# Two transformer blocks on one core: the weight halves and two token buffers placed at other addresses in SBUF

## The chip, the cores and the metric

One NeuronCore of a Trainium2 chip runs the whole program. The metric is the device time of one execution in microseconds, as the median of several runs.

## What is computed

The reference takes x (256 tokens of 2048 features, float32) through two blocks.

The first block is RMS norm, stick-breaking attention with 16 heads of 128 (`w_qkv`, `w_o`), residual, RMS norm, an MLP `square(relu(h @ w1)) @ w2` with 8192 hidden features, residual, RMS norm.

The second block puts 16 meta tokens in front and computes `proj = hn @ w_in` (12288 wide), a causal pooling over windows of 2, 4, 8 and 16 tokens with a grouped product, a gated causal convolution with `conv_out_w`, sigmoid gates, `w_o`, residual, then `(silu(gate) * up) @ w_down` with 5632 hidden features, residual and a last RMS norm. Only the 256 tokens leave the kernel.

So the work is a chain of matrix products of 256 (or up to 272) tokens with 2048-wide inputs and outputs, and all weights are read once.

## The kernel before

**Tiling.** A weight matrix is walked in panels of 512 output columns. A panel has 4 chunks, each 512 rows by 512 columns, loaded by one DMA of 1 MB into one of four `raw` slots (partition = row within a tile of 128). A chunk has two units of two row tiles.

**Splitting.** Each float32 operand is used as a high part (type fp32r) and a low part, the rest. For each unit ACT copies `raw` to the slot `whi` (L564) and DVE writes `raw - whi` to `wlo` (L771); four slots each, used in turn, so that two chunks of a panel use slots 0 and 1 and the other two use 2 and 3. The tokens lie likewise as high and low halves in `a_buf`, `b_buf`, `c_buf` and `d_buf`. A product is high x high + high x low + low x high: three matmuls for each weight tile, the function chunk().

**Three forms of a chunk.** A paired kind (attention's output and MLP products, gates and so on) loads a 128x128 tile of `whi` and moves the high and the low half of a token tile in one matmul of 2 x 256 = 512 columns (L1327, 16 matmuls in a row, the "high run"), then loads a tile of `wlo` and moves the 256 columns of the high half (L1334, 16 in a row, the "low run"). A kind that isn't paired does it unit by unit: 8 high and 8 more with the low tokens (L1374), then 8 with `wlo` (L1382), 256 to 272 columns each. The kinds `v`, `sum` and `fin` turn it round: the token tile is loaded and 512 columns of `whi` (L1355, 8 in a row) or `wlo` (L1361, 4 in a row) are moved. `last` does the same in L1484 and L1489.

**Who reads which buffer.** `a_buf` holds the input of q, k and v and of the second block's input projection; it has 272 columns a tile (16 meta tokens ahead), and its readers begin 16 columns in. `b_buf` holds the attention's output, the first MLP's hidden features, the pooled and the gated convolution features and the input of gate and up; `c_buf` the inputs of w1 and of the second block's w_o; `d_buf` the hidden features of the last MLP. `a_buf`, `c_buf` and `d_buf` share one stretch of memory at different times.

**Order.** Each engine has its own program, written out stage by stage in make_stages(); semaphores tie them. PE runs the chunks in that order without choice. place() gives each tensor its address within a partition: one after the other from `top[0]`, or at a given one. PE's tiles are read as 128 consecutive columns (512 bytes) for the load, and 1024 bytes, or twice 1024, or 2048 for the moving side:

```python
size = (size + 31) // 32 * 32
off = top[0] if at is None else at
if at is None:
    top[0] += size
```

In bytes from the base of the first tensor, which is a multiple of 64, before and after the change:

| tensor | size | before | after |
|---|---|---|---|
| raw | 32768 | 0 | 0 |
| whi | 16384 | 32768 | 49216 |
| wlo | 16384 | 49152 | 32768 |
| a_buf | 34816 | 65536 | 65600 |
| c_buf | 32768 | 65600 | 65728 |
| d_buf | 32768 | 65536 | 65600 |
| b_buf | 32768 | 100416 | 100416 |
| h and all that follows | | 133184 | 133184 |

A slot of whi or wlo has 4096 bytes, a row tile in it 2048, a 128-column tile 512. A token tile has 1088 bytes in a_buf and 1024 in the others; the low half begins 16 tiles behind the high one.

Of the kernel before, what the change touches and what calls it, by code (L numbers as in the profile page):

```python
# [18 lines left out]
F32R = mybir.dt.float32r  # L19

P = 128
D = 2048
NT = D // P
T = 256
# [7 lines left out]
PW = 512  # L32
# [8 lines left out]
UK = 2  # L41
UNITS = KT // UK
SPLIT = 4
# [204 lines left out]
def build(nc, x, meta, norm_mix, norm_mlp, final_norm, w_qkv, w_o1, w1, w2, norm_mix_2, w_in, b_gate,  # L248
# [6 lines left out]
    with ExitStack() as ctx:  # L255
        top = [(nc.sbuf_base + 63) // 64 * 64]
        arena_bytes = 0

        def place(name, shape, dt=F32, at=None):
            size = 4  # L260
            for s in shape[1:]:
                size *= s
# [4 lines that stand above are left out]
            return nc.alloc_sbuf_tensor_at(name, shape, dt, offset=off), off  # L267
# [3 lines left out]


        raw, _ = place("raw", [P, RAW, KT, PW])
        whi, _ = place("whi", [P, SPLIT, UK, PW], F32R)
        wlo, _ = place("wlo", [P, SPLIT, UK, PW], F32R)
        a_buf, a_off = place("a_buf", [P, 2, NT, TW], F32R)
        c_buf, _ = place("c_buf", [P, 2, NT, T], F32R, at=a_off + 64)
        d_buf, _ = place("d_buf", [P, 2, NT, T], F32R, at=a_off)
        top[0] += 64
        b_buf, b_off = place("b_buf", [P, 2, NT, T], F32R)  # L280
        a_hi, a_lo, b_hi, b_lo = a_buf[:, 0], a_buf[:, 1], b_buf[:, 0], b_buf[:, 1]
        c_hi, c_lo, d_hi, d_lo = c_buf[:, 0], c_buf[:, 1], d_buf[:, 0], d_buf[:, 1]
        h, _ = place("h", [P, NT, T])
        full, _ = place("full", [P, JT, T])
# [3 lines left out]
        acc, _ = place("acc", [P, JT, T])  # L288
        rr, _ = place("rr", [P, TW])
        rr1, _ = place("rr1", [P, T])  # L290
        ms, _ = place("ms", [P, 2, TW])
        msum = rr[:, 0:M]
        meta_f = rr1[:].rearrange("p (t n) -> p t n", n=M)
        vec, _ = place("vec", [P, 176])
        ident, _ = place("ident", [P, P])
        ones, _ = place("ones", [P, P])
        negtri, _ = place("negtri", [P, P], F32R)
        negone, _ = place("negone", [P, P], F32R)
        stat, _ = place("stat", [P, 24])
# [4 lines left out]
        za, _ = place("za", [P, NT, T])  # L304
        G, _ = place("G", [P, NT, TW])
        at = region
        k_hi, _ = place("k_hi", [P, JT, T], F32R, at=at)
        k_lo, _ = place("k_lo", [P, JT, T], F32R, at=at + 4096)
        v_hi, _ = place("v_hi", [P, MT, PW], F32R, at=at + 8192)
        v_lo, _ = place("v_lo", [P, MT, PW], F32R, at=at + 12288)  # L310
        t1, _ = place("t1", [P, GH, 3 * P], at=at + 16384)
        pp, p_off = place("pp", [P, 2, GH, 3 * P], F32R, at=at + 22528)
        p_hi, p_lo = pp[:, 0], pp[:, 1]
        t2, _ = place("t2", [P, GH, 3 * P], at=u_off)
# [4 lines left out]
        x_tok, _ = place("x_tok", [P, MT, D], at=region)  # L319
        meta_tok, _ = place("meta_tok", [M, D], at=region + 16384)  # L320
        x_sq, _ = place("x_sq", [P, MT, D], at=b_off)
        gm, _ = place("gm", [NT, P], at=region + 24576 + 1536)
        gv, _ = place("gv", [96, 2, P], at=region + 24576)
        tri32, _ = place("tri32", [P, P], at=region + 24576 + 1024)

        y_tok, _ = place("y_tok", [P, MT, D], at=region)
        g_rows, _ = place("g_rows", [P, D], at=region + 16384)
# [1246 lines left out]
```

How the kernel before makes its waits and increments, by code:

```python
        @block.sync  # L462
# [29 lines left out]
            def body(st, i):  # L492
# [3 lines left out]
                    n = cnt.n["chunk"]  # L496
                    if n < CH and st.iters == 1:
                        if n > 0:
                            load_x(n + 2)
                        load_halves(n)
                        cnt.n["chunk"] += 1
                        continue
                    if n == RAW:
                        load_vectors()
                    if st.iters > 1 or n >= RAW:
                        sp.wait_ge(w_lo, cnt.at("chunk", 1 - RAW) * UNITS)
                    if st.name == "dn_2" and k == 0 and c == 0:
                        sp.dma_start(g_rows[:], norm_final_2.unsqueeze(0).to_broadcast([P, D])).then_inc(g_landed, 16)
                    r = p.row0 + c * KT * P
# [12 lines left out]
                            start = cnt.n["chunk"]  # L522
                            cnt.per = {"chunk": sum(p.chunks for p in st.panels)}
                            body(st, i)
                        cnt.i = None
                        cnt.n["chunk"] = start + st.iters * cnt.per["chunk"]
            loops()
            for m in range(MT):
                for n, cols in enumerate((slice(3 * PW, D), slice(0, 2 * PW))):
                    sp.wait_ge(scaled_dve, 2 * m + n + 1)
                    sp.dma_start(out[0, m * P:(m + 1) * P, cols], y_tok[:, m, cols]).then_inc(stored, 16)
            sp.wait_ge(stored, 16 * 3 * MT)
# [127 lines left out]
            def h_out(g):  # L662
                act.wait_ge(h_turned, g + 1)
                b = 2 + 4 * (g % 2)
```

## Time and profile before

| | |
|---|---|
| median of 3 runs | 2592.38 us (2592.32 to 2592.49) |
| the profiled execution | 2592.15 us |
| its span | 2590.4 us |
| PE busy | 2580.2 us (100%), 16053 matmuls |
| PE weight load busy | 2321.9 us (90%) |
| DVE, ACT, POOL busy | 1614.6, 1174.1, 141.4 us |
| DMA | 485.26 MB, mean 187 GB/s |

PE is the matmul engine and PEld its loads of weights. A matmul's busy time is modelled and contains the latency of the array, so neighbours overlap in it: the pace of a stretch is read from the starts of its rows. The timeline merges like instructions into one row with the start of the first, the stretch from there to the end of the last, and their count; cut by a window, a row counts only the instructions that touch the window.

### The profile page before, as it was taken

The page shows a single profiled execution, that of the slowest core. Times are in us where ns is not written, and L with a number is a line of the kernel's source. Part 1 is how long each engine was busy: PE and PEld are TensorE (multiplying, and loading weights), DVE is VectorE, ACT ScalarE, POOL GpSimd, SP SyncE. Part 2 cuts the span into 40 slices and gives each one's busy share as a digit, 9 for nine tenths or more (in the row PEclk, how much of TensorE's full clock was granted, in tenths as well). Part 3 has the DMA queues.
Part 4 walks back from the last instruction along what each step waited for, and adds up shares of the span by engine and source line. Part 5 has one row for each costly group of instructions (what it writes and reads, how often), then busy time and mean ns, then how long its engine had stood idle before and what let it go on. Part 6 is the DMA issues. An engine that isn't in the chain of part 4 may idle for free.

```text
span 2590.4 us, 40378 instructions
## 1 busy us (share of the span) xinstructions
PE 2580.2 (100%) x16053; PEld 2321.9 (90%) x16053; DVE 1614.6 (62%) x1398; ACT 1174.1 (45%) x1181; POOL 141.4 (5%) x87
## 2 busy tenths in 40 slices
PE   9999999999999999999999999999999999999998
PEld 9999998888888888899899988888888888888887
DVE  6577766655556556886654776566756545554555
ACT  5455554434434444544533344444544434443444
POOL 0000100000000000000200530000000000000001
PEclk9999999999999999999999999999999999999999
DMA  7554455655655565555555555555555555555563
GB/s 263 180 171 157 162 182 191 193 186 190 195 190 185 192 195 189 184 179 186 188 181 189 182 181 193 188 186 194 194 184 190 181 192 194 189 190 191 191 211 130
DMA packets 243954, 485.26 MB, mean 187 GB/s; under 512 B 7728, under 2 KB 8944, under 8 KB 243696
## 3 DMA queue, kind: packets, MB, share of 16 engines
q1 hardware_dynamic: 243520, 483.12, 57.2%
q8 instruction: 82, 1.34, 0.2%
q10 hardware_dynamic: 320, 0.53, 0.1%
q14 instruction: 32, 0.26, 0.0%
HBM read 481.53 MB, written 2.10 MB: 187 GB/s over the span
## 4 chain that ended last, share of the span: by engine, by line
PE 99%; DVE 1%; issue 0%; ACT 0%; POOL 0%; DVEq 0%; POOLq 0%; ACTq 0%
PE ps L1327 42%; PE ps L1334 21%; PE ps L1374 14%; PE ps L1355 8%; PE ps L1382 7%; PE ps L1361 4%; PE ps L1430 0%; PE ps L1484 0%; PE ps L1396 0%; PE ps L1418 0%; PE ps L1257 0%; PE ps L1267 0%; PE ps L1489 0%; PE ps L1467 0%; PE ps L1421 0%
## 5 line engine op out<-in xcount | busy, mean ns | idle before, releaser
L771 DVE TENSOR_TENSOR wlo<-raw,whi 128x1024 fp32r<-128x1024 f32 x900 | 1107.8, 1262 | 923.9 <-ACT whi L564 923.8
L564 ACT ACTIVATE whi<-raw 128x1024 fp32r<-128x1024 f32 x900 | 919.3, 1054 | 1328.3 <-PE ps L1334 893.9
L1327 PE MATMUL ps<-b_buf,whi 128*128 128x512 f32 x2688 | 643.7, 392 | 0.0
L1327 PEld LDWEIGHTS ps<-b_buf,whi 128*128 128x128 f32 x2688 | 492.9, 188 | 97.6
L1334 PEld LDWEIGHTS ps<-b_buf,wlo 128*128 128x128 f32 x2688 | 334.9, 188 | 14.0
L1334 PE MATMUL ps<-b_buf,wlo 128*128 128x256 f32 x2688 | 337.9, 278 | 0.0
L1374 PE MATMUL ps<-a_buf,whi 128*128 128x258 f32 (+4 forms) x2560 | 330.9, 282 | 0.0
L1374 PEld LDWEIGHTS ps<-a_buf,whi 128*128 128x128 f32 x2560 | 315.7, 188 | 0.5 <-ACT a_buf L581 0.2
L1327 PE MATMUL ps<-c_buf,whi 128*128 128x512 f32 x1280 | 306.6, 392 | 0.0
L1327 PEld LDWEIGHTS ps<-c_buf,whi 128*128 128x128 f32 x1280 | 234.7, 188 | 46.4
L1327 PE MATMUL ps<-a_buf,whi 128*128 128x512 f32 x768 | 185.9, 394 | 0.0
L1382 PE MATMUL ps<-a_buf,wlo 128*128 128x258 f32 (+4 forms) x1280 | 179.8, 283 | 0.0
L1327 PEld LDWEIGHTS ps<-a_buf,whi 128*128 128x128 f32 x768 | 141.0, 188 | 29.7
L1355 PE MATMUL ps<-whi,d_buf 128*128 128x512 f32 x672 | 166.6, 390 | 0.0
L1334 PEld LDWEIGHTS ps<-c_buf,wlo 128*128 128x128 f32 x1280 | 159.4, 188 | 6.7
L1382 PEld LDWEIGHTS ps<-a_buf,wlo 128*128 128x128 f32 x1280 | 163.9, 188 | 0.5 <-DVE wlo L798 0.5
L1334 PE MATMUL ps<-c_buf,wlo 128*128 128x256 f32 x1280 | 160.9, 278 | 0.0
L1355 PEld LDWEIGHTS ps<-whi,d_buf 128*128 128x128 f32 x672 | 125.6, 188 | 25.9
L1334 PEld LDWEIGHTS ps<-a_buf,wlo 128*128 128x128 f32 x768 | 97.1, 188 | 4.1
L1334 PE MATMUL ps<-a_buf,wlo 128*128 128x256 f32 x768 | 98.2, 280 | 0.0
L1361 PE MATMUL ps<-wlo,d_buf 128*128 128x512 f32 x336 | 89.8, 389 | 0.0
L1374 PE MATMUL ps<-b_buf,whi 128*128 128x256 f32 x640 | 81.8, 279 | 0.9 <-DVE za L986 0.9
(202 smaller groups left out, 1473.0 us busy)
## 6 DMA issues: line engine op xcount, KB each, us to landing
raw<-in_mlp_w_dram SPq DMA_DIRECT2D x128, 1024.0 KB, 5.2
raw<-in_w_in_dram SPq DMA_DIRECT2D x96, 1024.0 KB, 5.0
raw<-in_w_gate_up_dram SPq DMA_DIRECT2D x88, 1024.0 KB, 5.0
raw<-in_sb_w_qkv_dram SPq DMA_DIRECT2D x44, 1024.0 KB, 5.1
raw<-in_w_down_dram SPq DMA_DIRECT2D x44, 1024.0 KB, 5.1
raw<-in_sb_w_o_dram SPq DMA_DIRECT2D x16, 1024.0 KB, 5.1
raw<-in_conv_out_w_dram SPq DMA_DIRECT2D x16, 1024.0 KB, 5.1
raw<-in_w_o_dram SPq DMA_DIRECT2D x16, 1024.0 KB, 5.1
```

What stands on the lines that cost most here:

```text
L564: act.activation(whi[:, unit_of(n, u)], raw[:, n % RAW, u * UK:(u + 1) * UK, :], ACT.Copy).then_inc(w_hi, 1)
L771: dve.tensor_tensor(wlo[:, s], raw[:, n % RAW, u * UK:(u + 1) * UK, :], cast(whi[:, s]), ALU.subtract).then_inc(w_lo, 1)
L1327: pe.matmul(ps[:, 4 * half + j, :].rearrange("p (a n) -> p a n", a=2), whi[:, s, kt, j * P:(j + 1) * P], buf[:, :, x, tok], start=c == 0 a ...
L1334: last = pe.matmul(ps[:, 4 * half + j, T:2 * T], wlo[:, s, kt, j * P:(j + 1) * P], hi[:, x, tok], start=False, stop=c == p.chunks - 1 and ...
L1355: pe.matmul(ps[:, 4 * half + m, :], part[:, x, toks[m]], whi[:, s, kt, :], start=first and kt == 0 and part is hi, stop=False, skip_group_ ...
L1361: last = pe.matmul(ps[:, 4 * half + m, :], hi[:, x, toks[m]], wlo[:, s, kt, :], start=False, stop=stop and kt == UK - 1, skip_group_check= ...
L1374: pe.matmul(outs[j], whi[:, s, kt, j * P:(j + 1) * P], part[:, x, tok], start=first and kt == 0 and part is hi and (wide_ or j % 2 == 0), ...
L1382: last = pe.matmul(outs[j], wlo[:, s, kt, j * P:(j + 1) * P], hi[:, x, tok], start=False, stop=stop and kt == UK - 1, skip_group_check=True)
```

## The change

The low parts `wlo` are placed in front of `whi`, and 64 bytes are left free between them. `a_buf` and `d_buf` thereby move 64 bytes up, the free 64 bytes in front of `b_buf` go, so that `b_buf` stays, and `c_buf` lies 128 bytes behind the start of `a_buf` instead of 64. No instruction is changed.

```diff
         raw, _ = place("raw", [P, RAW, KT, PW])
+        wlo, _ = place("wlo", [P, SPLIT, UK, PW], F32R)
+        top[0] += 64
         whi, _ = place("whi", [P, SPLIT, UK, PW], F32R)
-        wlo, _ = place("wlo", [P, SPLIT, UK, PW], F32R)
         a_buf, a_off = place("a_buf", [P, 2, NT, TW], F32R)
-        c_buf, _ = place("c_buf", [P, 2, NT, T], F32R, at=a_off + 64)
+        c_buf, _ = place("c_buf", [P, 2, NT, T], F32R, at=a_off + 128)
         d_buf, _ = place("d_buf", [P, 2, NT, T], F32R, at=a_off)
-        top[0] += 64
         b_buf, b_off = place("b_buf", [P, 2, NT, T], F32R)
```

## Rows read from the trace of the kernel before

**Rows 1.** The page: granted clock in 40 slices, and the chain by line.
```profile
PEclk9999999999999999999999999999999999999999
...
PE ps L1327 42%; PE ps L1334 21%; PE ps L1374 14%; PE ps L1355 8%; PE ps L1382 7%; PE ps L1361 4%; PE ps L1430 0%; PE ps L1484 0%; PE ps L1396 0%; PE ps L1418 0%; PE ps L1257 0%; PE ps L1267 0%; PE ps L1489 0%; PE ps L1467 0%; PE ps L1421 0%
```

**Rows 2.** Waits of PE, longest total first: total us, times, longest us.
```profile
PE ps L1257 <- POOL ident L1160: 1.6, 1, 1.6
```

**Rows 3.** Groups of matmuls by shape, whole span: busy us, mean ns, idle before.
```profile
L1327 PE MATMUL ps<-b_buf,whi 128*128 128x512 f32 x2688 | 643.7, 392 | 0.0
L1327 PE MATMUL ps<-c_buf,whi 128*128 128x512 f32 x1280 | 306.6, 392 | 0.0
L1355 PE MATMUL ps<-whi,d_buf 128*128 128x512 f32 x672 | 166.6, 390 | 0.0
L1374 PE MATMUL ps<-b_buf,whi 128*128 128x256 f32 x640 | 81.8, 279 | 0.9 <-DVE za L986 0.9
```

**Rows 4.** Timeline of PE, 2031 to 2036 us: the first runs with d_buf.
```profile
2031.14 2.00 PE L1355 MATMUL ps<-whi,d_buf 128*128 128x512 f32 x8
2032.98 1.07 PE L1361 MATMUL ps<-wlo,d_buf 128*128 128x512 f32 x4
2033.89 1.98 PE L1355 MATMUL ps<-whi,d_buf 128*128 128x512 f32 x8
2035.70 0.62 PE L1361 MATMUL ps<-wlo,d_buf 128*128 128x512 f32 x2
```

**Rows 5.** Timeline of PE, 489 to 501 us: two paired chunks with b_buf.
```profile
489.14 3.82 PE L1327 MATMUL ps<-b_buf,whi 128*128 128x512 f32 x16
492.80 2.04 PE L1334 MATMUL ps<-b_buf,wlo 128*128 128x256 f32 x16
494.69 3.84 PE L1327 MATMUL ps<-b_buf,whi 128*128 128x512 f32 x16
498.37 1.98 PE L1334 MATMUL ps<-b_buf,wlo 128*128 128x256 f32 x16
500.18 3.82 PE L1327 MATMUL ps<-b_buf,whi 128*128 128x512 f32 x16
```

**Rows 6.** By tile, last matmul of both high runs: duration ns min/median/max, starts.
```profile
L1327 PE MATMUL ps<-b_buf,whi x1: 388/388/388, 492.6 to 492.6; 128*128 128x512 f32 x1
...
L1327 PE MATMUL ps<-b_buf,whi x1: 394/394/394, 498.1 to 498.1; 128*128 128x512 f32 x1
```

**Rows 7.** Timeline of PE, 1219 to 1225 us: a paired chunk with a_buf.
```profile
1219.21 3.87 PE L1327 MATMUL ps<-a_buf,whi 128*128 128x512 f32 x16
1222.92 2.05 PE L1334 MATMUL ps<-a_buf,wlo 128*128 128x256 f32 x16
1224.80 1.55 PE L1327 MATMUL ps<-a_buf,whi 128*128 128x512 f32 x6
```

**Rows 8.** Timeline of PE, 337 to 338 us: the attention's product with v.
```profile
337.29 0.64 PE L1440 MATMUL ps<-pp,v_hi 128*128 128x256 f32 x4
337.77 0.56 PE L1430 MATMUL ps<-pp,v_lo 128*128 128x128 f32 x4
```

**Rows 9.** Timeline: the 5th, 9th and 13th matmul of rows 7's high run.
```profile
1220.12 0.40 PE L1327 MATMUL ps<-a_buf,whi 128*128 128x512 f32 x1
...
1221.06 0.39 PE L1327 MATMUL ps<-a_buf,whi 128*128 128x512 f32 x1
...
1221.99 0.39 PE L1327 MATMUL ps<-a_buf,whi 128*128 128x512 f32 x1
```

**Rows 10.** Timeline of PE, 133 to 134 us: a low run of v with a_buf.
```profile
133.11 1.08 PE L1361 MATMUL ps<-wlo,a_buf 128*128 128x512 f32 x4
134.03 0.62 PE L1355 MATMUL ps<-whi,a_buf 128*128 128x512 f32 x2
```

**Rows 11.** Timeline of PE, 1292 to 1296 us: the grouped product with b_buf.
```profile
1291.92 1.99 PE L1374 MATMUL ps<-b_buf,whi 128*128 128x256 f32 x16
1293.74 1.07 PE L1382 MATMUL ps<-b_buf,wlo 128*128 128x256 f32 x8
```

## The prediction, made before the changed kernel ran

> **What bounds the kernel now.** I read the page first [rows 1]: TensorE's clock is granted at 9 tenths or more in every slice, and of the chain that ended last six lines of PE, L1327, L1334, L1374, L1355, L1382 and L1361, the matmuls of the weight chunks, hold 96%. Then the waits of PE: the longest in the whole span is 1.6 us, at the start [rows 2]. So PE neither waits for a tile nor runs on a lowered clock; only a change of its own pace can move the time. The conversions on ACT and DVE that write whi and wlo, and the DMAs, stand nowhere on that chain.
>
> Third, the pace. The trace's duration of a matmul contains a constant latency, so I take starts: the start of one run of 16 to the start of the next, by 16. For one and the same shape this pace differs with the tensor it reads, and that is what the change touches.
> - 512 columns with d_buf: 8 matmuls from 2033.89 to 2035.70 and 4 from 2032.98 to 2033.89, 226 to 227 ns each [rows 4], the lowest pace of the shape.
> - 512 columns with b_buf: 3.66 or 3.68 us for 16, 229 ns [rows 5], and the last matmul of the one lasts 388 ns, of the other 394 [rows 6]: the price goes round in a pattern instead of settling.
> - 512 columns with a_buf: 3.71 us, 232 ns [rows 7].
> - 256 columns: 1.81 us for 16 (113 ns) or 1.89 (118 ns) with b_buf [rows 5], 1.88 with a_buf [rows 7], and 0.48 for 4 (120 ns) in the attention's product of v with pp [rows 8].
> DVE, ACT and the DMAs come and go under these runs, and the runs repeat to 0.01 us. So it isn't traffic. I read it as a clash inside PE's own two readers, the load of the next weights and the stream of the moving tile, which depends on the distance of the two addresses.
>
> Distances (moving start minus loaded start, modulo 256 bytes), from the sizes in place(): b_buf and c_buf stand 64 from whi and from wlo. d_buf stands 0 from both. Tile x of a_buf stands 64(x+1) from both, since its rows are 1088 bytes and the tokens begin 64 bytes in. pp and v stand 0. I choose 256 because the quarters of a high run of a_buf (four matmuls each, at 64, 128, 192 and 0) take 0.91, 0.94, 0.93 and 0.93 us [rows 9]: 128 and 0 are not alike, if weakly.
>
> **What the change moves.** No instruction, wait or DMA is added, removed or reordered; the tiles from b_buf on keep their addresses. New distances: b_buf to whi 0 (was 64), to wlo 64 (kept). c_buf to whi 128, to wlo 192. d_buf to whi 0 (kept), wlo to d_buf 192 (was 0). a_buf to whi kept, to wlo 64 more. The sum goes part by part, against the profiled execution (2592.15 us around a span of 2590.4, 0.2 below the median shown, so nothing to correct).
>
> *b_buf in pairs, 168 chunks* (2688 matmuls by 16 [rows 3]). Now two chunks take 5.55 and 5.49 us, 5.52 each [rows 5]. The high run at distance 0 should settle as d_buf's does: 16 x 0.2266 = 3.626. It has to settle anew in each chunk, though: the first run with d_buf after one with b_buf takes 1.84 us for 8 and the next one 1.81 [rows 4], so +0.03. Now the low run, whose distance is kept. It has two paces, and the row before it decides: after a high run of 3.66 it takes 1.89, after one of 3.68 it takes 1.81 [rows 5]. They alternate because the high run's pattern doesn't close in 16. A high run that settles hands over the same state each time, so the low runs will be all fast or all slow. A chunk costs 3.626 + 0.03 + 1.885 = 5.541 (slow) or 5.466 (fast). I take slow: the low run is slow after the high run whose last matmul was a cheap one of 388 ns [rows 5, 6], and a settled run ends on cheap ones. That is +0.021 x 168 = +3.5 us. Ends: fast and no resettling, -0.08 x 168 = -13; a_buf's pace, 5.59 a chunk [rows 7], +12.
>
> *c_buf, 80 chunks* (1280 by 16 [rows 3]). At distance 128 the row nearest is a_buf's second quarter, 0.94 for four [rows 9]: 3.76 for 16, and with a low run of 1.88 [rows 7] 5.64, +0.12 a chunk, +9.6 us. If 128 acts as 0 it is b_buf's +0.021, +1.7. a_buf's whole chunk, through all distances, is +0.07. I take +0.05, between b_buf's and a_buf's: +4.0 us. Lower end as for b_buf, -6.
>
> *d_buf, 84 units* (672 by 8 [rows 3]). The four low matmuls lose the distance at which they settle; with a_buf the same form takes 0.92 [rows 10] against 0.91, and the next high run has to resettle (+0.03). +0.04 x 84 = +3.3 us; ends 0 and 4.5, should the high run not settle within its 8 matmuls.
>
> *b_buf, not in pairs, 20 chunks* (640 by 32 [rows 3]): high matmuls of 256 columns at distance 0, which is what the attention's v and pp have, 120 ns [rows 8], against 118 in the output projection (its group's mean is 279 ns [rows 3], that of a slow run) and 1.82 us for 16, 113 ns, in three chunks of the grouped product [rows 11]. 512 x 0.0023 + 96 x 0.0067 + 48 x 0.0044 = 1.2 + 0.6 + 0.2 = +2.0 us; ends -4 (all at 113) and +3.
>
> *a_buf, 144 chunks*: its high distances stay, the low ones swap places among the same four. Mean 0, +-3 us.
>
> Sum: 3.5 + 4.0 + 3.3 + 2.0 + 0 = +12.8, 2605 us.
>
> **Rivals.**
> 1. *Low runs all fast* (the other side of zero). Same mechanism as above, other branch: the settled high run hands over the state that the 3.68 run hands over. For it: the grouped product keeps its 113 ns for whole chunks [rows 11], so the fast pace can hold for good; two states, and I know the end of neither. Against: the order in [rows 5]. Price: (5.466 - 5.520) x 248 = -13.4, with d_buf's 3.3 and 1 for the rest, -9: 2583 us. It decides at the first low matmul after a settled run.
> 2. *No change*: the address doesn't matter to PE, and the paces differ by something else that goes with the tensor (tile stride, pattern of two halves). Then 2592.4. Against it: paired b_buf and a_buf have the same pattern of halves and differ, 3.67 to 3.71. This time would also come out if the parts cancel. The Trainium skill states this as a rule: SBUF — State Buffer, section "Who interferes with whom", gives PE two independent read ports, one for the moving operand and one for the weight load, and says "PE and ACT never wait on anyone". By that rule the placement is free and the time stays; it says nothing of PE's two readers clashing with each other, and [rows 5, 7] with their two paces for one shape speak against reading it so.
> 3. *c_buf dear*: 128 and 192 bytes hold the high run at 0.94 for four or worse for all 16. 3.5 + 9.6 + 4.5 + 2.0 + 1 = +21, 2613 us.
>
> **How the numbers follow.** Forecast 0.46, rival 1 0.24, rival 2 with cancelling 0.18, rival 3 0.12. A difference of 0.2% (5.2 us) is about what can be told from none here. Faster 0.24; the same 0.19 (rival 2 and a little of the forecast's lower end); slower 0.57. The range from 2582 to 2616 takes in rivals 1 and 3 at their own prices; the likeliest case alone is 2598 to 2611.
>
> **What would show it.** Right: high runs of b_buf at 3.65 to 3.66 with the last matmuls at 389 ns, each followed by a low run of 1.88; c_buf's chunks above 5.53 and now unlike b_buf's; wlo with d_buf above 0.91 and the high run behind it at 1.84; the attention's own matmuls unchanged. Wrong: low runs of 1.81 in every chunk (rival 1); b_buf at 229 ns as before (rival 2, or the two readers don't clash); c_buf at or below 5.47, which would say that 64 or 128 is the modulus and that the +128 is harmless. A wait of PE above a few us anywhere would be a mechanism that I haven't in the sum.

## The result and the profile after

The changed kernel takes 2609.11 us (2608.89 to 2609.32, four runs) against 2592.43 us (2592.32 to 2592.58) for the kernel before beside it: ratio 1.0064, 95% interval 1.0051 to 1.0077. It is slower by 16.7 us; 12.8 were forecast, with 2605 us, and the range of 2582 to 2616 holds the time.

First the page of the changed kernel, with the longest group of waits, as long as in [rows 2]. The span is 2607.2 us, 16.8 longer.
```profile
PEclk9999999999999999999999999999999999999999
...
PE ps L1327 42%; PE ps L1334 21%; PE ps L1374 14%; PE ps L1355 8%; PE ps L1382 7%; PE ps L1361 4%; PE ps L1484 0%; PE ps L1430 0%; PE ps L1396 0%; DMA raw<-in_sb_w_qkv_dram 0%; PE ps L1418 0%; PE ps L1489 0%; PE ps L1467 0%; PE ps L1421 0%;
...
PE ps L1257 <- POOL ident L1160: 1.6, 1, 1.6
```
Clock, chain and longest wait answer to [rows 1, 2] without a difference. One wait of PE changed, the one for za, from 0.9 us [rows 3] to 0.5. The 16.8 us were spent inside the same matmuls, at the same clock. The groups by shape (busy us, mean ns of one, idle before), against [rows 3]:
```profile
L1327 PE MATMUL ps<-b_buf,whi 128*128 128x512 f32 x2688 | 646.9, 393 | 0.0
L1327 PE MATMUL ps<-c_buf,whi 128*128 128x512 f32 x1280 | 310.4, 395 | 0.0
L1355 PE MATMUL ps<-whi,d_buf 128*128 128x512 f32 x672 | 168.0, 392 | 0.0
L1374 PE MATMUL ps<-b_buf,whi 128*128 128x256 f32 x640 | 83.5, 283 | 0.5 <-DVE za L986 0.5
```
Each mean has grown by 1 to 4 ns. A mean contains the latency, so it shows only the direction. For sizes I add up start to next start, per line and tile, over the whole span:

| matmuls | before | after | difference | forecast |
|---|---|---|---|---|
| b_buf paired, high (L1327) | 616.44 | 619.68 | +3.2 | |
| b_buf paired, low (L1334) | 310.67 | 316.53 | +5.9 | together +3.5 |
| c_buf (L1327, L1334) | 441.56 | 445.88 | +4.3 | +4.0 |
| d_buf (L1355, L1361, and the last product L1484, L1489) | 239.73 | 243.70 | +4.0 | +3.3 |
| b_buf not in pairs, high (L1374) | 75.33 | 76.97 | +1.6 | |
| b_buf not in pairs, low (L1382) | 38.60 | 36.93 | -1.7 | together +2.0 |
| a_buf (all six lines) | 817.03 | 816.36 | -0.7 | 0 |
| everything else on PE | 42.04 | 42.05 | 0.0 | 0 |

The sum is +16.7. In the -1.7 of the unpaired low runs, 0.4 is the shorter wait for za, which stands behind one of them; their pace gives -1.3. Now the runs behind these totals. Timeline of PE in the changed kernel (start us, us with the latency, count), paired chunks with b_buf, against [rows 5]:
```profile
493.91 2.05 PE L1334 MATMUL ps<-b_buf,wlo 128*128 128x256 f32 x16
495.79 3.85 PE L1327 MATMUL ps<-b_buf,whi 128*128 128x512 f32 x16
499.48 2.05 PE L1334 MATMUL ps<-b_buf,wlo 128*128 128x256 f32 x16
501.37 3.85 PE L1327 MATMUL ps<-b_buf,whi 128*128 128x512 f32 x16
505.06 2.05 PE L1334 MATMUL ps<-b_buf,wlo 128*128 128x256 f32 x16
```
By starts: high 3.69, low 1.88 or 1.89, and no alternation is left. Before, each second low run took 1.81. The last matmul of a high run, by tile (duration min/median/max), is a cheap one, as in the first line of [rows 6]:
```profile
L1327 PE MATMUL ps<-b_buf,whi x1: 388/388/388, 493.7 to 493.7; 128*128 128x512 f32 x1
```
Two chunks with c_buf:
```profile
807.76 3.87 PE L1327 MATMUL ps<-c_buf,whi 128*128 128x512 f32 x16
811.47 2.05 PE L1334 MATMUL ps<-c_buf,wlo 128*128 128x256 f32 x16
813.36 3.88 PE L1327 MATMUL ps<-c_buf,whi 128*128 128x512 f32 x16
817.08 1.98 PE L1334 MATMUL ps<-c_buf,wlo 128*128 128x256 f32 x16
818.90 3.87 PE L1327 MATMUL ps<-c_buf,whi 128*128 128x512 f32 x16
```
Here the two chunks differ as before (5.60 and 5.54), but both high runs take 3.71 or 3.72. The runs with d_buf, against [rows 4]:
```profile
2040.81 2.03 PE L1355 MATMUL ps<-whi,d_buf 128*128 128x512 f32 x8
2042.67 1.10 PE L1361 MATMUL ps<-wlo,d_buf 128*128 128x512 f32 x4
2043.61 2.00 PE L1355 MATMUL ps<-whi,d_buf 128*128 128x512 f32 x8
2045.44 1.10 PE L1361 MATMUL ps<-wlo,d_buf 128*128 128x512 f32 x4
```
The low run has gone from 0.91 to 0.94 and the high run behind it from 1.81 to 1.83. Last the grouped product, whose b_buf isn't read in pairs:
```profile
1304.10 2.08 PE L1374 MATMUL ps<-b_buf,whi 128*128 128x256 f32 x16
1306.02 1.07 PE L1382 MATMUL ps<-b_buf,wlo 128*128 128x256 f32 x8
1306.93 2.08 PE L1374 MATMUL ps<-b_buf,whi 128*128 128x256 f32 x16
```
1.92 for the 16 high ones, 120 ns each as with v and pp [rows 8], and 0.91 for the 8 low ones, 113 ns.

### The profile page after: what moved, and what is told of

It reads as the page before. It is cut to its first block, busy times and chain, and to the rows that moved or that the text cites. A ratio compares the mean times of both kernels' runs of the same rounds, so it can differ in the third digit from the quotient of the medians.

```text
span 2607.2 us, 40378 instructions
## 1 busy us (share of the span) xinstructions
PE 2597.3 (100%) x16053; PEld 2329.1 (89%) x16053; DVE 1614.1 (62%) x1398; ACT 1174.3 (45%) x1181; POOL 141.2 (5%) x87
## 4 chain that ended last, share of the span: by engine, by line
PE 98%; DVE 1%; DMA 0%; ACT 0%; issue 0%; POOL 0%; SPq 0%; DVEq 0%; ACTq 0%; POOLq 0%
PE ps L1327 42%; PE ps L1334 21%; PE ps L1374 14%; PE ps L1355 8%; PE ps L1382 7%; PE ps L1361 4%; PE ps L1484 0%; PE ps L1430 0%; PE ps L1396 0%; DMA raw<-in_sb_w_qkv_dram 0%; PE ps L1418 0%; PE ps L1489 0%; PE ps L1467 0%; PE ps L1421 0%; DVE wlo L771 0%
## 5 line engine op out<-in xcount | busy, mean ns | idle before, releaser
L1327 PE MATMUL ps<-b_buf,whi 128*128 128x512 f32 x2688 | 646.9, 393 | 0.0
L1327 PEld LDWEIGHTS ps<-b_buf,whi 128*128 128x128 f32 x2688 | 493.2, 188 | 102.2
L1334 PEld LDWEIGHTS ps<-b_buf,wlo 128*128 128x128 f32 x2688 | 340.0, 188 | 12.8
L1334 PE MATMUL ps<-b_buf,wlo 128*128 128x256 f32 x2688 | 344.0, 279 | 0.0
L1374 PE MATMUL ps<-a_buf,whi 128*128 128x258 f32 (+4 forms) x2560 | 332.4, 282 | 0.1
L1374 PEld LDWEIGHTS ps<-a_buf,whi 128*128 128x128 f32 x2560 | 316.9, 188 | 0.6 <-ACT a_buf L581 0.3
L1327 PE MATMUL ps<-c_buf,whi 128*128 128x512 f32 x1280 | 310.4, 395 | 0.0
L1327 PEld LDWEIGHTS ps<-c_buf,whi 128*128 128x128 f32 x1280 | 235.6, 188 | 49.3
L1327 PE MATMUL ps<-a_buf,whi 128*128 128x512 f32 x768 | 185.0, 392 | 0.0
L1382 PE MATMUL ps<-a_buf,wlo 128*128 128x258 f32 (+4 forms) x1280 | 179.2, 282 | 0.0
L1355 PE MATMUL ps<-whi,d_buf 128*128 128x512 f32 x672 | 168.0, 392 | 0.0
L1327 PEld LDWEIGHTS ps<-a_buf,whi 128*128 128x128 f32 x768 | 140.6, 188 | 28.8
L1334 PEld LDWEIGHTS ps<-c_buf,wlo 128*128 128x128 f32 x1280 | 159.8, 188 | 6.9
L1382 PEld LDWEIGHTS ps<-a_buf,wlo 128*128 128x128 f32 x1280 | 163.8, 188 | 0.3 <-DVE wlo L798 0.2
L1334 PE MATMUL ps<-c_buf,wlo 128*128 128x256 f32 x1280 | 161.4, 279 | 0.0
L1355 PEld LDWEIGHTS ps<-whi,d_buf 128*128 128x128 f32 x672 | 125.6, 188 | 28.6
L1334 PEld LDWEIGHTS ps<-a_buf,wlo 128*128 128x128 f32 x768 | 96.6, 188 | 4.1
L1334 PE MATMUL ps<-a_buf,wlo 128*128 128x256 f32 x768 | 97.3, 279 | 0.0
L1361 PE MATMUL ps<-wlo,d_buf 128*128 128x512 f32 x336 | 91.9, 394 | 0.0
L1374 PE MATMUL ps<-b_buf,whi 128*128 128x256 f32 x640 | 83.5, 283 | 0.5 <-DVE za L986 0.5
```

What stands on the lines that cost most here:

```text
L1327: pe.matmul(ps[:, 4 * half + j, :].rearrange("p (a n) -> p a n", a=2), whi[:, s, kt, j * P:(j + 1) * P], buf[:, :, x, tok], start=c == 0 a ...
L1334: last = pe.matmul(ps[:, 4 * half + j, T:2 * T], wlo[:, s, kt, j * P:(j + 1) * P], hi[:, x, tok], start=False, stop=c == p.chunks - 1 and ...
L1355: pe.matmul(ps[:, 4 * half + m, :], part[:, x, toks[m]], whi[:, s, kt, :], start=first and kt == 0 and part is hi, stop=False, skip_group_ ...
L1361: last = pe.matmul(ps[:, 4 * half + m, :], hi[:, x, toks[m]], wlo[:, s, kt, :], start=False, stop=stop and kt == UK - 1, skip_group_check= ...
L1374: pe.matmul(outs[j], whi[:, s, kt, j * P:(j + 1) * P], part[:, x, tok], start=first and kt == 0 and part is hi and (wide_ or j % 2 == 0), ...
L1382: last = pe.matmul(outs[j], wlo[:, s, kt, j * P:(j + 1) * P], hi[:, x, tok], start=False, stop=stop and kt == UK - 1, skip_group_check=True)
```

## The experiments

In what follows a pair such as 64/64 is the distance of a chunk's high run (moved tile minus loaded tile, modulo 256; with b_buf and c_buf that is the token tile minus whi) and of its low run (the same with wlo). Run times are from start to next start.

**Order alone.** The two weight tensors change places, and every distance is kept modulo 256.
```diff
+        wlo, _ = place("wlo", [P, SPLIT, UK, PW], F32R)
         whi, _ = place("whi", [P, SPLIT, UK, PW], F32R)
-        wlo, _ = place("wlo", [P, SPLIT, UK, PW], F32R)
```


> wlo placed ahead of whi, and nothing else: no 64 bytes between them, c_buf 64 past a_buf, b_buf at its place. Theory (PE's pace depends on the distance between the tile it moves and the tile it loads, modulo 256 bytes): all distances are what they were in the kernel before (16384 is a multiple of 256), so 2592.4 us within 0.3, the paired chunks of b_buf again 5.55 and 5.49 us in turn. Rival (the order, or a distance modulo something larger than 256 bytes, counts): a difference of several us, up to the 16.7 of the whole change.

Measured: 2592.27 us against 2592.10, ratio 1.0001 (0.9992 to 1.0011). The two chunks of [rows 5] stand at the same times, with the same alternation:
```profile
489.14 3.82 PE L1327 MATMUL ps<-b_buf,whi 128*128 128x512 f32 x16
492.80 2.05 PE L1334 MATMUL ps<-b_buf,wlo 128*128 128x256 f32 x16
494.69 3.84 PE L1327 MATMUL ps<-b_buf,whi 128*128 128x512 f32 x16
498.36 1.98 PE L1334 MATMUL ps<-b_buf,wlo 128*128 128x256 f32 x16
```
So "the low parts lie in front" costs nothing. All of the change is in its 64 and 128 bytes.

**Everything moved by 64 bytes.** 64 bytes of room ahead of raw, the first tensor; negtri and negone go into the memory of S1 to make place for it.
```diff
+        top[0] += 64
         raw, _ = place("raw", [P, RAW, KT, PW])
...
-        negtri, _ = place("negtri", [P, P], F32R)
-        negone, _ = place("negone", [P, P], F32R)
+        negtri, _ = place("negtri", [P, P], F32R, at=s1_off + 2048)
+        negone, _ = place("negone", [P, P], F32R, at=s1_off + 2560)
```


> Everything from raw on stands 64 bytes higher, distances as in the kernel before (the two constant matrices of the attention's suffix sums moved into free room to make space). Theory (distances alone count): 2592.4 us within 0.5. Rival (the address itself counts, as b_buf at phase 64 and whi at phase 0 in the kernel before): another time by more than 2 us, and other paces in the paired chunks.

Measured: 2592.2 us, ratio 1.0000 (0.9990 to 1.0009). So the address itself doesn't count; only a difference between tensors can.

**A scan of pairs, in four kernels.** Each stage group reads its own b_buf, set off by so many bytes, and so eight pairs are seen in one kernel. The first, with low at the same distance as high:
```diff
+        top[0] += 256
         a_buf, a_off = place("a_buf", [P, 2, NT, TW], F32R)
-        c_buf, _ = place("c_buf", [P, 2, NT, T], F32R, at=a_off + 64)
-        d_buf, _ = place("d_buf", [P, 2, NT, T], F32R, at=a_off)
-        top[0] += 64
+        c_buf, _ = place("c_buf", [P, 2, NT, T], F32R, at=a_off + 224)
+        c_late, _ = place("c_late", [P, 2, NT, T], F32R, at=a_off + 160)
+        d_buf, _ = place("d_buf", [P, 2, NT, T], F32R, at=a_off + 128)
         b_buf, b_off = place("b_buf", [P, 2, NT, T], F32R)
+        b_pa, _ = place("b_pa", [P, 2, NT, T], F32R, at=b_off + 0)
+        b_pb, _ = place("b_pb", [P, 2, NT, T], F32R, at=b_off + 64)
+        b_pc, _ = place("b_pc", [P, 2, NT, T], F32R, at=b_off + 128)
+        b_pd, _ = place("b_pd", [P, 2, NT, T], F32R, at=b_off + 192)
...
```
The dots stand for two more buffers, at 32 and 96, and for the lines that let each stage pick its buffer. The other three kernels do the same with wlo moved against whi.

> A scan in one run: the hidden features of the four quarters of the first MLP, the convolution's output product and gate/up read b_buf's data at 0, 64, 128, 192, 32 and 96 bytes of distance, to whi and wlo alike; c_buf at 224 (MLP) and 160 (w_o of the second block), d_buf 128 the other way. Theory: the pace goes by distance modulo 256: at 64 the high run 3.66 and 3.68 and the low run 1.89 and 1.81 in turn as before; at 0 the high run settles (3.65 to 3.70) and the low run is 1.92 (120 ns, as v with pp); at 128 and 192 the high run is 3.70 or more. Rival (modulo 128): 128 like 0 and 192 like 64. Rival (the tensor and not the distance counts): 5.52 us a chunk in all.

> The same scan with the low parts' distance 64 more than the high parts': pairs (high, low) of 0/64, 64/128, 128/192, 192/0 in the quarters of the first MLP, 32/96 in the convolution's output product, 224/32 in gate/up; c_buf 96/160 and 160/224. Theory: 0/64 repeats the changed kernel's b_buf (3.69 and 1.884, 5.573 a chunk) and 128/192 its c_buf (3.708 and 3.722, 1.887 and 1.822); the others are unknown, between 5.44 and 5.70. Rival (something else of the changed layout slowed b_buf): 0/64 comes out otherwise.

> whi stays at the phase of a_buf, wlo lies 128 bytes past it (mod 256); eight places of the hidden features and gates give the pairs (high run's distance / low run's distance) 0/128, 64/192, 128/0, 192/64 and 32/160, 96/224, 160/32, 224/96. Theory (the pace of a run is set by its own distance modulo 256 and by what the run before it left): high runs at 0 take 3.65 to 3.69 us, at 64 3.66 to 3.70, at 128 3.70 to 3.73, at 192 3.73 to 3.74; low runs at 0 1.88 to 1.92, at 64 1.83 to 1.89, at 128 1.88 to 1.90, at 192 1.82 to 1.90. No pair under the 5.52 us of before's 64/64, so the kernel is slower than before: about 2615 to 2625 us. Rival A (runs don't act on each other, each distance has one duration): the high run at 0 would be 3.65 again as in 0/0 or 3.69 as in 0/64, and one of the two is already excluded. Rival B (a pair is cheap when both runs lie in the same relation to each other, high minus low equal 0): every pair here is above 5.60 us.

> wlo lies 64 bytes past whi, so the low run's distance is 64 less than the high run's: pairs 0/192, 64/0, 128/64, 192/128 and 32/224, 96/32, 160/96, 224/160. Theory (own distance and what the run before left): high runs as in the scans before (0: 3.65 to 3.69 us, 64: 3.66 to 3.70, 128: 3.70 to 3.73, 192: 3.73 to 3.74), low runs 1.82 to 1.92; a pair with a high run at 0 or 64 (3.65 to 3.67) and a low run of 1.82 would be 5.47 to 5.49 and beat before's 5.52, which would be worth up to 0.05 x 168 = 8 us. Rival (the low run is fast, 113.3 ns a matmul, only where it lies at the same distance as the high run ahead of it): every pair is 5.53 or more and the best stays before's. Whole kernel about 2610 to 2625 us, since only one quarter of the stages lies at each pair.

Measured: 2625.65, 2620.39, 2622.94 and 2624.86 us, one run each. Mean of a chunk in us (high + low run), a row for each distance of the high run:

| high | low 0 | low 64 | low 128 | low 192 |
|---|---|---|---|---|
| 0 | 3.653+1.913 = 5.566 | 3.685+1.884 = 5.569 | 3.643+1.924 = 5.567 | 3.652+1.886 = 5.538 |
| 64 | 3.660+1.913 = 5.573 | 3.669+1.853 = **5.522** | 3.674+1.893 = 5.567 | 3.727+1.881 = 5.608 |
| 128 | 3.717+1.904 = 5.621 | 3.709+1.884 = 5.593 | 3.724+1.899 = 5.623 | 3.716+1.854 = 5.570 |
| 192 | 3.738+1.896 = 5.634 | 3.724+1.882 = 5.606 | 3.722+1.898 = 5.620 | 3.731+1.823 = 5.554 |

The sixteen pairs at odd multiples of 32 take 5.600 to 5.663. Out of the first scan, a chunk and the next high run, at 0/0 and at 128/128:
```profile
542.98 3.82 PE L1346 MATMUL ps<-b_pa,whi 128*128 128x512 f32 x16
546.63 2.08 PE L1353 MATMUL ps<-b_pa,wlo 128*128 128x256 f32 x16
548.55 3.82 PE L1346 MATMUL ps<-b_pa,whi 128*128 128x512 f32 x16
...
900.95 3.88 PE L1346 MATMUL ps<-b_pc,whi 128*128 128x512 f32 x16
904.67 2.06 PE L1353 MATMUL ps<-b_pc,wlo 128*128 128x256 f32 x16
906.57 3.90 PE L1346 MATMUL ps<-b_pc,whi 128*128 128x512 f32 x16
```
0 and 128 differ by 0.06 a chunk, 64 and 192 by 0.03: 128 is not the modulus. 512 isn't either, nor a larger power of two: by the addresses the first scan's b_pa lies 265 x 256 bytes behind whi, and the b_buf of the kernel "b_buf alone" below lies 264 x 256 behind it, and both have high runs of 3.65 us and low runs of 1.91. So the distance counts modulo 256. The first scan's b_pb repeats the kernel before, the second one's b_pa and b_pc the changed kernel's b_buf and c_buf (5.569 and 5.570 against 5.573 for either). So the tensor and the stage don't matter.

The last two expectations missed in part. I had given each distance of a high run one price, but 64 costs 3.66 ahead of a low run at 0 and mostly 3.736 ahead of one at 192 (the low run at 0/128, 1.924, lies above its 1.88 to 1.90 too):
```profile
715.73 2.04 PE L1354 MATMUL ps<-b_pb,wlo 128*128 128x256 f32 x16
717.61 3.90 PE L1347 MATMUL ps<-b_pb,whi 128*128 128x512 f32 x16
721.35 2.04 PE L1354 MATMUL ps<-b_pb,wlo 128*128 128x256 f32 x16
```
(the third scan, 64/192). Fifteen of its 16 steps from start to start are a level 232 to 234 ns, where in 64/64 the differences go 226, 229, 232 round and round. So one distance has more than one steady pattern: at 64/192 the first two high runs take 3.66 us and the other fourteen 3.736. That the run before selects the pattern fits this, but isn't shown by it alone. I had also hoped for 5.47 to 5.49 in the fourth scan. The time of its rival came instead: no pair is under 5.53, and the kernel before keeps the best. The rival's reason doesn't hold, though: the changed kernel's c_buf, at 128/192, has a low run of 1.82 every second time, and the two distances aren't equal there.

**c_buf at its phase.** The changed kernel with c_buf at 0/64.
```diff
-        c_buf, _ = place("c_buf", [P, 2, NT, T], F32R, at=a_off + 128)
+        c_buf, _ = place("c_buf", [P, 2, NT, T], F32R, at=a_off + 0)
```


> The changed kernel with c_buf at the phase of a_buf instead of 128 bytes past it: its runs go from the pair 128/192 to 0/64. Theory: a c chunk then takes what b_buf's chunks take in the changed kernel, 3.689 + 1.884 = 5.573 us, in place of 3.715 + 1.855 = 5.570: 80 chunks x 0.003 = 0.2 us, so no difference to the changed kernel, 2609.4 us, ratio 1.0065 to before. Rival A (c_buf's offset is what made the change dear, c_buf past its phase): the time falls by the 4.3 us that c cost, to 2605. Rival B (the tensor and what lies behind it matter, not the distance): c's runs keep 3.708/3.722 and 1.887/1.822.

Measured: 2609.24 us (2609.0 to 2609.6), ratio 1.0066 (1.0049 to 1.0083), where the table gave 2609.4. c_buf's chunks have become b_buf's:
```profile
808.23 3.85 PE L1327 MATMUL ps<-c_buf,whi 128*128 128x512 f32 x16
811.92 2.05 PE L1334 MATMUL ps<-c_buf,wlo 128*128 128x256 f32 x16
813.80 3.85 PE L1327 MATMUL ps<-c_buf,whi 128*128 128x512 f32 x16
```
The 128 bytes past the phase are thus not dearer than no offset at all (rival A, 2605, falls, and rival B with it); c_buf's +4.3 us are what it costs to leave 64/64.

**b_buf alone.** The kernel before without its 64 bytes of room: b_buf at 0/0. What lies behind it moves down with it by 64 bytes, all else is as it was.
```diff
         d_buf, _ = place("d_buf", [P, 2, NT, T], F32R, at=a_off)
-        top[0] += 64
         b_buf, b_off = place("b_buf", [P, 2, NT, T], F32R)
```


> The kernel before with b_buf alone moved 64 bytes down (its line of 64 bytes of room deleted): b's runs go from the pair 64/64 to 0/0, all else stays. Theory: 168 paired chunks from 5.522 to 5.566 = +7.4 us; 40 unpaired high runs from 1.883 to 1.924 = +1.6 and 40 low runs from 0.965 to 0.971 = +0.2: together +9.2, 2601.6 us, ratio 1.0035. Rival A (only the relation of low to high matters, which stays 0): no change, 2592.4. Rival B (the high run costs at 0 what it costs in the changed kernel, 3.689, and the low run is as fast as in before): +0.019 x 168 = +3.2, 2595.6.

Measured: 2603.27 us (2603.1 to 2603.4), ratio 1.0043 (1.0026 to 1.0060), 11.2 above the 2592.07 beside it. 9.2 were expected. Rival A (no change) and rival B (2595.6) fall. By the starts: paired b_buf 168 x (5.567 - 5.518) = +8.2, high runs not in pairs 40 x 0.041 = +1.6, their low runs 40 x 0.006 = +0.2 (+0.8 of pace, less a wait for za that is 0.6 shorter), and c_buf, whose place is untouched, 80 x 0.009 = +0.7. That is 10.7. The expected 7.4 used the scan's 5.522 for 64/64, in place of the whole kernel's 5.518. Most important is the low run, now also at 0:
```profile
495.21 2.08 PE L1333 MATMUL ps<-b_buf,wlo 128*128 128x256 f32 x16
497.12 3.82 PE L1326 MATMUL ps<-b_buf,whi 128*128 128x512 f32 x16
500.77 1.48 PE L1333 MATMUL ps<-b_buf,wlo 128*128 128x256 f32 x11
```
The high run is cheaper than before on average (3.65 against 3.67), the low run dearer by more (1.91 against 1.85).

**Every run twice, changed kernel.** Paired chunks issue their 16 high matmuls twice and their 16 low ones twice, so that each run is seen behind the other kind and behind its own; the products of these stages count double.
```diff
+                    for u, s, kt, x in units:
+                        for j in range(JT):
+                            pe.matmul(ps[:, 4 * half + j, :].rearrange("p (a n) -> p a n", a=2),
+                                      whi[:, s, kt, j * P:(j + 1) * P], buf[:, :, x, tok],
+                                      start=False, stop=False, skip_group_check=True)
...
```


> The changed kernel with every run of a paired chunk issued twice: 16 high matmuls, the same 16 again, 16 low ones, the same 16 again (so the products of these stages count twice). It shows each run behind another kind and behind its own kind. Theory (b_buf's high run at distance 0 loses 62 ns because it settles anew behind each low run): first high run 3.689 us, second 3.627 (226.7 ns a matmul, d_buf's pace), the two low runs 1.884 each, since a pace once handed over stays. c_buf at 128/192: the high run doesn't settle, 3.70 to 3.72 both times. Kernel: +168 x 5.511 + 80 x 5.57 + 48 x 5.55 = 1638 us, 4247 us. Rival A (the pace at distance 0 is 230.6 ns with these tensors and there is no settling): 3.689 both times, +10 us, 4257. Rival B (the low run's pace is set by its distance alone, not by what it takes over): can't be told here if both stay at 1.884; it is the kernel before with its runs twice that tells it.

Measured: 4243.16 us. L1327 is the first high run, L1332 the second, L1339 and L1345 the low ones:
```profile
689.62 3.84 PE L1327 MATMUL ps<-b_buf,whi 128*128 128x512 f32 x16
693.29 3.79 PE L1332 MATMUL ps<-b_buf,whi 128*128 128x512 f32 x16
696.92 2.04 PE L1339 MATMUL ps<-b_buf,wlo 128*128 128x256 f32 x16
698.80 2.04 PE L1345 MATMUL ps<-b_buf,wlo 128*128 128x256 f32 x16
700.69 3.84 PE L1327 MATMUL ps<-b_buf,whi 128*128 128x512 f32 x16
```
The first takes 3.67, the second 3.63 (means of 168: 3.672 and 3.626). 3.626 is 16 times 226.6 ns, d_buf's pace [rows 4]. So a run at distance 0 does reach that pace with b_buf, and what it pays above it is paid behind a low run. It isn't a price of the distance alone (rival A, 3.689 twice). The two low runs stay alike at 1.88. c_buf at 128/192 doesn't gain by its second run: 3.714 and 3.720.

**Every run twice, kernel before.** The same edit at 64/64.

> The kernel before with every run of a paired chunk issued twice (the products of these stages count twice): b_buf and c_buf at 64/64. Theory: at 64 the high run has a pattern that goes round, so the second high run costs what the first does, 3.66 to 3.68 us; the low run's pace (1.81 or 1.88) is handed over to it by the high run, and the second low run behind a low run keeps the pace of the first: pairs of 1.813 + 1.813 and 1.884 + 1.884. Kernel: +168 x 5.52 + 80 x 5.52 + 48 x 5.59 = 1637 us, 4230 us. Rival A (every run settles behind its own kind, and 64 has a floor too): the second high run at 3.63, the second low run at 1.81 always. Rival B (the low run's two paces alternate by themselves): 1.813 followed by 1.884 within a chunk.

Measured: 4225.45 us. Two neighbouring chunks:
```profile
695.27 2.05 PE L1339 MATMUL ps<-b_buf,wlo 128*128 128x256 f32 x16
697.16 2.05 PE L1345 MATMUL ps<-b_buf,wlo 128*128 128x256 f32 x16
699.04 3.83 PE L1327 MATMUL ps<-b_buf,whi 128*128 128x512 f32 x16
702.71 3.83 PE L1332 MATMUL ps<-b_buf,whi 128*128 128x512 f32 x16
706.37 1.98 PE L1339 MATMUL ps<-b_buf,wlo 128*128 128x256 f32 x16
708.19 1.98 PE L1345 MATMUL ps<-b_buf,wlo 128*128 128x256 f32 x16
710.00 3.82 PE L1327 MATMUL ps<-b_buf,whi 128*128 128x512 f32 x16
```
A low run behind a low run keeps its pace: 1.89 then 1.88, or 1.82 then 1.81; in all 168 chunks the two differ by 0.003 us at most. It is the high run that hands the pace over, and the low run keeps it through both runs. The second high run costs what the first does (3.664 and 3.662): at 64 there is nothing to settle into. Both rivals fall. Both whole times came out some 4 us below their sums.

No version beats the kernel before: its 64/64 is the cheapest of the 32 pairs seen for b_buf and c_buf, and 0/0 is the cheapest of those seen for d_buf (its 8 high ones take 1.82 us there, and 1.84 at 0/192, 1.85 at 64/0 and 1.86 at 128/128).

## Why the forecast held, and where it was off

- *What bounds the kernel.* Right: no wait, no clock, no traffic; the 16.7 us are the paces of PE's matmuls, less the 0.4 us of one shorter wait. The kernels with order and address changed alone exclude both of these, and the scan shows that it's the distance of the two addresses. That the two readers clash is read from this distance; it isn't seen directly.
- *b_buf's low run always slow.* Right: each of 168 low runs takes 1.884 (+5.9 us together). Rival 1, all fast, needed 1.81. It decided the sign in my sum, but not in the kernel: with the other parts as measured, fast low runs would have given 168 x 0.071 = 11.9 us less, and the change would still have cost about 5 us (an estimate from these rows). Handing over, which was argued from the order in [rows 5], is shown by the doubled runs.
- *b_buf's high run.* This step failed in size. It was to settle at 226.6 ns after a loss of 0.03, taken from d_buf's first run [rows 4]. It does settle, but the 16 steps from start to start of the run at 501.37 us, the last one to the low run (ns, worked out from the trace), are
```
241 237 234 236 224 231 235 229 232 231 227 226 227 227 226 226
```
  so it takes ten matmuls and 0.062 us. The run from which I took 0.03 is no measure of that: its steps are 231 236 228 233 230 227 227 226, so it had settled by its sixth matmul, from another starting point. The trace before also held the longer way, in the high run with d_buf at 2037.40 us, behind eight transposes: 314 234 236 224 231 235 229 232, the same values as above and not settled at its end. So the loss hangs on what the run takes over. In the scan it is 0.059 at 0/64, and 0.027, 0.017 and 0.026 at 0/0, 0/128 and 0/192: my 0.03 would have done for these three. With 0.062 the chunk is 3.689 + 1.884 = 5.573 in place of 5.541, and 168 x 0.032 is 5.4 us. The forecast's +3.5 and these 5.4 make 8.9 of the 9.1 measured. The doubled kernel shows the same term from the other side: 3.626 when nothing has to settle. There the loss behind two low runs is 0.046.
- *c_buf.* +4.3 for +4.0, but by luck: between 0.02 and 0.12 a chunk I chose 0.05, and 0.054 came. That 128 isn't a cheap distance was right (3.72); that the low run at 192 would be fast every second time was not foreseen. Rival 3 fell.
- *d_buf.* +4.0 for +3.3. The low run costs 0.934, more than a_buf's 0.92 [rows 10]; the high run pays 0.018 on average, less than the 0.03 taken. (0.04 x 84 is 3.4, not 3.3.)
- *b_buf not in pairs.* Wrong, by 2 us: the high matmuls rose to 120 ns as argued from v and pp [rows 8], +1.6, but behind them the low runs of eight fell from 0.942 to 0.907, -1.3, and the wait for za among them grew shorter, -0.4. Together this took the rise back. I had left their pace out of the account, though I had argued for the paired chunks that a run hands its state on. With b_buf alone at 0/0 they stand at 0.960. The counts were off too: 512 + 96 + 48 is more than the 640 high matmuls, and what the 48 are isn't said. And the trace has the 113 ns in two chunks of the grouped product, not in three: behind the wait of 0.90 us PE goes on at 118 ns. This also weakens what rival 1 drew from it, that the fast pace can hold for good.
- *a_buf.* -0.7, inside the +-3, as a remainder of parts that cancel: the paired chunks give -1.9, the rest +1.2. Their high runs went from 3.711 to 3.691 us though no high distance changed, which fits a pace handed on by the low runs between them and wasn't in the sum.
- *Rival 2, no change.* Excluded by the interval. The Trainium skill (SBUF — State Buffer, "Who interferes with whom") gives PE two independent read ports, one for the moving operand and one for the weight load, and says that PE never waits on anyone. Where that is read to mean that placement costs nothing, the measurement decides against it: in the scan one and the same run of 16 takes 3.64 to 3.75 us by the addresses alone.

The signs that I had named came, but for one: the low runs of 1.88, c_buf above 5.53 and unlike b_buf in its runs (in sum both take 5.573), wlo with d_buf above 0.91 and its high run at 1.84, the attention's matmuls unchanged. b_buf's high run was to take 3.65 to 3.66 and takes 3.69.

The result was 4 us above the forecast. The step that failed is the price of settling in b_buf's high run, 0.03 us taken and 0.062 measured: it alone is +5.4, and the -2 of the unpaired runs and small terms took a part back.

## What to carry to other kernels

Where PE never waits and the clock is full, compare the pace of one matmul shape across the tensors that it reads, by starts and not by durations: a difference of 1 or 2% that goes with the tensor can be the placement of the moving tile against the loaded one, and it is worth moving a buffer by 64 bytes, one at a time. Don't judge a distance by its settled pace. The 226.6 ns of distance 0 is the lowest pace seen here for 512 columns, and yet 64 with its 229 won. At 0 the high run of 16 pays 0.02 to 0.06 us to settle behind each low run, and at 0/0, where it is still the cheaper one (3.65 against 3.67), the low run costs more than that gains (1.91 against 1.85). Take the cost of a transition from one that begins behind the same kind of run, or give it a range; here it went from 0.017 to 0.062 us.

## What was not expected of the hardware

- The pace depends on what ran before, and not on the distance alone. Low runs at distance 64 take 113.3 or 117.8 ns a matmul, for 32 in a row if nothing comes between, by what the high run ahead left. For the high shape at 64 two steady patterns were seen, 229 and 233.5 ns on average.
- The cost isn't the same function of the distance for the two shapes: a high run costs 3.63 us settled at 0, and on average 3.66 to 3.73 at 64, 3.71 to 3.72 at 128 and 3.72 to 3.74 at 192; the means of low runs range from 1.82 (192/192) to 1.92 (0/128).
- At odd multiples of 32 bytes every pair is dearer than 64/64, by 0.08 to 0.14 us a chunk.
- Why the distance of the two addresses matters stays open: no run here looks inside PE's reads.
